# A hybrid attention block on one core: x scaled by ScalarE, its block sums on VectorE, the second burst of each head at job 9, two plain tiles after the last short jobs

## What is computed

```python
h = rmsnorm(x, g_norm)
z = h @ w_in                       # 2048 x 12296: per head q, k, v, gate; 8 forget logits; two merge gates
oa = differential attention of 8 heads (two softmax maps, partial rotary), rmsnorm, * silu(gate)
ob = forgetting attention of 8 heads (cumulative log-forget bias),          * silu(gate)
m = sigmoid(ma) * (oa @ w_proj_a) + sigmoid(mb) * (ob @ w_proj_b)
out = rmsnorm(x + m @ w_out, g_final)
```

## Time and profile before

| | |
|---|---|
| time, median of 3 runs | 762.02 us (760.89 to 762.63) |
| the profiled execution's own time | 762.58 us |
| its span, first to last instruction | 760.6 us |
| TensorE busy | 736.4 us, 97% of the span |
| VectorE, ScalarE, GpSimd busy | 77%, 56%, 14% |
| mean granted clock of TensorE | 0.994 of full speed |

### The profile page before, as it was taken

How to read it: one execution, slowest core, us unless ns; L and a number is a source line. 1 busy time by engine, 2 the same in 40 slices (tenths; PEclk the granted TensorE clock), 3 DMA queues, 4 the chain that set the end, 5 groups by cost and what they waited for, 6 DMA issues and landing times.

```text
span 760.6 us, 9798 instructions
## 1 busy us (share of the span) xinstructions
PE 736.4 (97%) x3536; PEld 611.5 (80%) x3536; DVE 582.7 (77%) x755; ACT 424.2 (56%) x624; POOL 108.4 (14%) x165
## 2 busy tenths in 40 slices
PE   8889999999999999999999999999998899999996
PEld 6678888888888888888887888887777688888886
DVE  6976688789769789778979877988997457665552
ACT  6555665555656565666565565656665343444541
POOL 0660212010000003120303020210020000001110
PEclk9999999999999999999999999999999899999999
DMA  8458646767866676776575767566767455855542
GB/s 321 124 192 280 247 173 218 252 213 265 280 230 222 214 256 230 255 264 221 198 270 193 254 230 285 198 228 204 253 206 246 137 177 198 325 191 190 189 148 111
DMA packets 47374, 168.97 MB, mean 222 GB/s; under 512 B 5400, under 2 KB 5408, under 8 KB 46816
## 3 DMA queue, kind: packets, MB, share of 16 engines
q1 hardware_dynamic: 46064, 164.97, 62.8%
q10 hardware_dynamic: 1008, 1.84, 0.7%
q0 software_dynamic: 256, 1.54, 0.5%
HBM read 166.23 MB, written 2.11 MB: 221 GB/s over the span
## 4 chain that ended last, share of the span: by engine, by line
PE 78%; DVE 11%; issue 3%; ACT 3%; DMA 3%; ACTq 0%; POOL 0%; DVEq 0%; POOLq 0%
PE Z L336 25%; PE Z L338 24%; PE Z L337 24%; DVE w_lo L831 5%; ACT w_hi L606 2%; PE A L438 1%; DMA w_raw<-in_w_main 1%; DMA x_sb<-in_xT 1%; DVE z_sb L884 1%; DVE w_raw L845 1%; DVE x_sb L847 1%; PE A L404 1%; PE B L420 1%; PE Dk L429 1%; PE B L417 1%
## 5 line engine op out<-in xcount | busy, mean ns | idle before, releaser
L831 DVE TENSOR_TENSOR w_lo<-w_raw,w_hi 128x1024 fp32r<-128x1024 f32 (+1 forms) x240 | 293.0, 1226 | 114.6 <-ACT w_hi L606 111.3
L606 ACT ACTIVATE w_hi<-w_raw 128x1024 fp32r<-128x1024 f32 (+1 forms) x235 | 243.7, 1043 | 204.4 <-PE Z L338 156.3
L336 PE MATMUL Z<-w_hi,hT_hi 128*128 128x512 f32 (+2 forms) x720 | 274.9, 382 | 6.5 <-DVE w_lo L831 5.0
L338 PE MATMUL Z<-w_hi,hT_lo 128*128 128x512 f32 (+2 forms) x720 | 272.8, 379 | 0.0
L337 PE MATMUL Z<-w_lo,hT_hi 128*128 128x512 f32 (+2 forms) x720 | 272.8, 379 | 0.0
L336 PEld LDWEIGHTS Z<-w_hi,hT_hi 128*128 128x128 f32 x720 | 135.3, 188 | 34.8 <-issue 6.1
L338 PEld LDWEIGHTS Z<-w_hi,hT_lo 128*128 128x128 f32 x720 | 135.3, 188 | 25.7
L337 PEld LDWEIGHTS Z<-w_lo,hT_hi 128*128 128x128 f32 x720 | 135.4, 188 | 24.4
L336 PE MATMUL Z<-w_hi,sum_hi 128*128 128x512 f32 x256 | 102.9, 402 | 7.0 <-DVE gates L868 5.0
L338 PE MATMUL Z<-w_hi,sum_lo 128*128 128x512 f32 x256 | 100.9, 394 | 0.0
L337 PE MATMUL Z<-w_lo,sum_hi 128*128 128x512 f32 x256 | 100.7, 393 | 0.0
(11 more groups left out here) (184 smaller groups left out, 603.2 us busy)
## 6 DMA issues: line engine op xcount, KB each, us to landing
w_raw<-in_w_main SPq DMA_DIRECT2D x283, 512.0 KB, 4.2
x_sb<-in_w_main SPq DMA_DIRECT2D x16, 512.0 KB, 7.5
w_raw<-in_w_fl SPq DMA_DIRECT2D x8, 264.0 KB, 3.1
o_T<-in_x SPq DMA_DIRECT2D x1, 2048.0 KB, 8.0
x_sb<-in_xT ACTq DMA_DIRECT2D x4, 256.0 KB, 7.9
x_sb<-in_xT SPq DMA_DIRECT2D x4, 256.0 KB, 5.4
gates<-c_rows_dram POOLq DMA_DIRECT2D x1, 1024.0 KB, 6.9
z_sb<-in_g_final SPq DMA_DIRECT2D x1, 1024.0 KB, 10.0
```

The source lines that it names most:

```text
L336: pe.matmul(acc, a_hi, b_hi, start=first, stop=False)
L338: return pe.matmul(acc, a_lo, b_hi, start=False, stop=last)
L606: act.activation(w_hi[:, t % RING, 0:cols_of(t)], weights(t), ACT.Copy).then_inc(hi_ready, 1)
L831: dve.tensor_tensor(w_lo[:, t % RING, 0:n], weights(t), w_hi[:, t % RING, 0:n].bitcast(fp32), ALU.subtract).then_inc(lo_ready, 1)
```

## The change

1. `x` is scaled by g on ScalarE (`x_scale`: 16 operations of 128x256, two after each split of jobs 8 to 15), and the four block sums are made by VectorE (`x_sums`, one after the split of job 18, three between and behind those of jobs 21, 22 and 23). GpSimd's twelve operations are gone.
2. Splitting these sums into `sum_hi`, `sum_lo` (`PARTS_AT`) moves from jobs 21 to 24 to jobs 27, 30, 39 and 46.
3. The burst Y of each head from 3 on moves from step 12 to step 9. What hangs on it moves along.
4. In the last mixed cycle the plain tiles stand at steps 0, 2, 4, 5, 8, 11, 14, 15 (before: 0, 2, 4, 5, 8, 10, 12, 13), the short jobs end at 13 (before: 15).
5. The split of `o_T` moves: part 0 four jobs earlier, parts 2 and 3 to jobs 255 and 256.

```diff
-FOX_STEPS, FOX_SUM_STEPS = (0, 2, 4, 5, 8, 10, 12, 13), (1, 3, 6, 7, 9, 11, 14, 15)
+FOX_STEPS, FOX_SUM_STEPS = (0, 2, 4, 5, 8, 11, 14, 15), (1, 3, 6, 7, 9, 10, 12, 13)
-Y_AT = {25: 0, 33: 1, 43: 2, **{MIXED_JOB + 16 * (b - 2) + 12: b for b in range(3, N_HEADS)}, FOX2_JOB + 5: N_HEADS}
+Y_AT = {25: 0, 33: 1, 43: 2, **{MIXED_JOB + 16 * (b - 2) + 9: b for b in range(3, N_HEADS)}, FOX2_JOB + 5: N_HEADS}
-O_SPLIT_AT = {FOX_JOB - 16: 0, FOX_JOB - 14: 1, FOX_JOB - 6: 2, FOX_JOB + 2: 3}
+PARTS_AT = {PLAIN_JOB + 7: 0, MIXED_JOB + 2: 1, MIXED_JOB + 11: 2, MIXED_JOB + 18: 3}
+O_SPLIT_AT = {FOX_JOB - 20: 0, FOX_JOB - 14: 1, FOX2_JOB + 3: 2, FOX2_JOB + 4: 3}
...
+            def x_scale(j):
+
+                for k in (2 * j, 2 * j + 1):
+                    act.wait_ge(xl_ready, k + 1)
+                    act.activation(xT_sb[:, k, :], xT_sb[:, k, :], ACT.Copy, scale=g_col[:, k:k + 1]).then_inc(h_scaled, 1)
...
                 split(FL_JOB + j)
+                x_scale(j)
...
+            def x_sums(form):
+
+                if form == SUM_1:
+                    dve.wait_ge(h_scaled, KT)
+                    a, b, op = xT_sb[:, near, tok1], xT_sb[:, far, tok1], ALU.add
...
+                dve.tensor_tensor(sums_raw[:, form], a, b, op).then_inc(sums_ready, 1)
...
             split(18)
+            x_sums(SUM_1)
...
             for t in range(PLAIN_JOB, PLAIN_JOB + RING):
                 split(t)
+                if t > PLAIN_JOB:
+                    x_sums((SUM_2, SUM_4, SUM_3)[t - PLAIN_JOB - 1])
...
-            for j in range(TILES):
-                pool.wait_ge(xl_ready, 2 * j + 2)
-                pool.wait_ge(x_squared, j + 1)
-                sl = slice(2 * j, 2 * j + 2)
-                pool.tensor_tensor(xT_sb[:, sl, :], xT_sb[:, sl, :], g_col[:, sl].unsqueeze(2).to_broadcast([P, 2, SEQ]),
-                                   ALU.mult).then_inc(h_scaled, 1)
```

More of the change, by code:

```diff
@@ L754, in _ @@
                 split(job + RING)
-                if PLAIN_JOB + 1 <= job < PLAIN_JOB + 5:
-                    sum_hi_part(job - PLAIN_JOB - 1)
+                if job in PARTS_AT:
+                    sum_hi_part(PARTS_AT[job])
                 attention(job)
@@ L884, in x_sum @@
                 dve.tensor_tensor(x_ssq, before, x_sq[:, 2 * j:2 * j + 2, :], ALU.add).then_inc(x_summed, 1)
+            def x_sums(form):
+                if form == SUM_1:
+                    dve.wait_ge(h_scaled, KT)
+                    a, b, op = xT_sb[:, near, tok1], xT_sb[:, far, tok1], ALU.add
+                elif form == SUM_2:
+                    a, b, op = sums_raw[:, SUM_1], xT_sb[:, near, tok0], ALU.subtract
+                elif form == SUM_4:
+                    a, b, op = xT_sb[:, far, tok0], sums_raw[:, SUM_2], ALU.subtract
+                else:
+                    a, b, op = xT_sb[:, near, tok0], xT_sb[:, near, tok1], ALU.subtract
+                if form in (SUM_2, SUM_4):
+                    dve.wait_ge(sums_ready, form)
+                dve.tensor_tensor(sums_raw[:, form], a, b, op).then_inc(sums_ready, 1)
             dve.memset(warm, 0.0).then_inc(warm_ready, 1)
@@ L1079, in _ @@
                     dve.tensor_scalar(c_neg[:], C[0:HEADS, 0:SEQ], -1.0, None, ALU.mult).then_inc(c_neg_ready, 1)
-                if PLAIN_JOB + 1 <= job < PLAIN_JOB + 5:
-                    sum_lo_part(job - PLAIN_JOB - 1)
+                if job in PARTS_AT:
+                    sum_lo_part(PARTS_AT[job])
                 attention(job)
```

## The result

The changed kernel took 752.69 us (median of 4 runs, 748.14 to 754.77) beside 761.65 us for the kernel before: a ratio of 0.987, 95% interval 0.983 to 0.992. It is faster by 9 us, 1.2%; the forecast was 745.8 us, 741 to 751. The profiled execution took 752.39 us, its span is 750.6 us.

A forecast was written before the change was run, and what follows sets the result against it. TensorE's own rate was taken to bound the steady state. Start 6.1, bursts 2.0 and last mixed cycle 8.1 us sum to 16.2 us off the 762.02 us median: 745.8 us, range 741 to 751 us.

The forecast's parts named there:

- The start: Kernel start, GpSimd's work moved to ScalarE and VectorE: 6.5 us won less a new wait of 0.4 us, 6.1 us.
- first 264-column matmul: Sign at the start: TensorE begins it near 30.3 us instead of 34.01 us, 3.7 us won.
- first 256-column one: Sign at the start: TensorE begins it near 43 us instead of 49.56 us, its wait of 2.81 us gone whole.
- the `c_nat` wait: End of job 21, before the `C` product: VectorE's block sums leave a new wait of 0.4 us.
- The last mixed cycle: Its end: no stop for the fold of P2 before job 252 and no lower clock, 8.1 us won.
- the fold ended 2.2 us ahead of job 252: Last mixed cycle: fold of P2 done 2.2 us before job 252 asks for it, formerly 5.02 us behind.
- The bursts: Burst Y at step 9: 4.5 us of old waits won, 2.5 us of new waits, net 2.0 us.
- The old waits: TensorE's waits at steps 3 and 4 of the next cycle: all go, 3.9 us plus slower first matmuls, 4.5 us.
- The evacuation is late: Next step 0 waits 0.5 us for VectorE's evacuation in cycles 7, 8, 10, 11 and 12: 2.5 us of new waits.
- the one-cycle clock: One differential head's cycle timed from TensorE's end of step 9; put the evacuation 0.3 us late for step 0.
- The slower one: Rival, burst at step 9: every evacuation late in 12 cycles, a loss from 1.6 us each, 767 us at 2 us; 3 in 100.

The follow-up runs named there:

- e4: Kernel before with only x scaled by ScalarE, block sums on VectorE and their later splits: 754.53 us, ratio 0.990.
- e7: Kernel before with only the last mixed cycle's new order of plain tiles and short jobs: 754.11 us, ratio 0.990.
- e1: Changed kernel with burst Y back at step 12, all other edits kept: 745.25 us, ratio 0.977.
- e3: Changed kernel with the differential heads' rotary step cut to one product per head (output lacks the rotation): 743.72 us, ratio 0.975.
- e6: Kernel before with only burst Y moved to step 9: 766.85 us, ratio 1.007.
- e10: Changed kernel with ScalarE evacuating both halves (heads 9 and up) and `combine_maps` four bodies behind Y instead of two: 747.3 us, ratio 0.981.
- e5: Changed kernel with ScalarE evacuating both halves of a differential head's tile (heads 9 and up): 741.71 us, ratio 0.974.
- e8: Changed kernel measured once more, nothing altered: 751.81 us (749.88 to 755.49), ratio 0.987.
- e2: Changed kernel with VectorE's normalizers and `combine_maps` four bodies behind Y instead of two, behind the evacuation: 744.41 us, ratio 0.976.

## Why the prediction was wrong

**The start, 6.1 us forecast: right in mechanism, mis-sized by 1.8 us.** e4 alone gives 7.9 us. `x_sum`, `half_rstd` and the split came back to the lengths that the undisturbed rows gave. TensorE's first 264-column matmul moved by 4.1 us and its first 256-column one by 7.2 us, for 3.7 and 6.5 forecast; 0.46 us of both stood already at 10.7 us, ahead of anything that the change touches. Two terms were mis-sized in the jobs behind: waits of 0.7 us at 56.54 us went too, which I had left out, and the `c_nat` wait, forecast at 0.4 us, measured about 0.1 us. Job 22 starts 7.7 us sooner (61.86 for 69.56). Single traces are good to half a microsecond here: the transposes behind job 21 start at 68.4 to 69.2 us in three kernels with the old start and at 60.7 to 61.9 us in ten with the new one. The extra 1.8 us was luck for the forecast: without it the whole would have been missed by more.

**The last mixed cycle, 8.1 us forecast: right.** e7 gives 7.8 us, and the traces of before and after differ by 7.9 us there. In the changed kernel the fold ended 2.2 us ahead of job 252, as laid out, and the clock held.

**The bursts, 2.0 us forecast: here it failed.** The two terms that stood in the sum were right. The old waits went, 4.9 us by the starts for 4.5 forecast. The evacuation is late in cycles 7, 8, 10, 11 and 12, the five forecast, by 0.46 us four times and 0.66 us once, 2.5 us for 2.5 forecast. (One reading was off without consequence: five of the twelve cycles, not six, have no `combine_maps`.) The step that failed is the one-cycle clock, where "VectorE then does its half" is followed down to the evacuation and no further: TensorE, ScalarE and VectorE were on that clock, and GpSimd was not, although `rope` of the next head waits for that same evacuation and the transposes at step 4 wait for `rope`. Its term was put at nothing without a reason.

What the runs showed in its place: `rope` costs 6.0 us of waits, 6.8 us by the starts of matmuls, and about 1.6 us of lower clock behind one of them. With it the bursts cost some 5.5 us instead of winning 2.0: the lead of the changed kernel's trace is 7.7 us at the transposes at 337.5 us, 2.2 us at those of the last head at 561.0 us, and 10.1 us at the end, behind the fold's 7.9 us; the profiled executions differ by 10.2 us. (The four terms, 4.9 - 2.5 - 6.8 - 1.6, make -6.0 us; the 0.5 us between was not followed.) e1 to e3 show that the missing term is `rope`: each takes the wait away by another road, and each is 7 to 9 us faster than the changed kernel.

The rows needed were in the trace of before: `rope` started right behind the evacuation, at 367.51 us, and ended near 373 us, 8 us ahead of the transposes at 381.0 us. That looks like ample slack. In the changed kernel `rope` starts 1.9 us later against the transposes, and its eight products take 8.1 us more, 11.87 for 3.78: it was mostly their length that used the slack up.

The Trainium skill has the rule for that, in "SBUF — State Buffer", "Who interferes with whom": a VectorE instruction with two inputs in SBUF contends with a GpSimd instruction that reads SBUF, and the pair of ports that the two share is an exclusive lock. The rows agree: a product takes 0.25 us when VectorE pauses or reads PSUM, and 1.18 to 1.23 us in the median beside a row of operations of 1.22 us. They go beyond it in one point: a product can wait past three such operations (3.38 us) or nine (9.59 us in e6). I used this contention for the start, in one direction, where GpSimd slowed VectorE, and did not ask what VectorE's new order does to GpSimd.

Of the rivals none was this one. The slower one named the late evacuation, with 1.6 us per head as the point from which it decides; e6 shows that the burst's move alone is in fact a loss of 4.9 us. The range missed by 1.7 us: it had no room for an engine that was not on the plan.

Open: what decides whether a product of GpSimd gets its turn after one of VectorE's operations or only after three or nine; and why e10 is slower than either of its cures, which only rows of one place suggest.

## What to carry to other kernels

When a burst of work moves, list every engine that waits for any of its results or for what is now queued behind it, the idle engines too: an engine at 14% busy sat on the critical path as soon as its 12 small operations per head ran beside an unbroken row of VectorE's two-input ones. A short wait in such a chain was cured here at its start (e5, 10 us better than the changed kernel in e8) or by putting operations that read PSUM, and a pause, beside the small ones (e2), and the two cures did not add up (e10). The bank last used before a row of long tiles was freed in time by putting other tiles behind its last use (e7), not by an earlier burst (e6).

## What was not expected of the hardware

- A GpSimd product of 128x32 takes 0.25 us when VectorE pauses or reads PSUM (e6: five of them in 1.11 us beside two folds) and 1.2 us beside VectorE's row of operations with both inputs in SBUF. It can wait past more than one of them: 3.38 us in the changed kernel, 9.59 us in e6, and in e3, where one product per head is left, 2.8 us in the median.
- The length of TensorE's stop alone does not tell whether its clock falls. Before the first 256-column matmul it stood 2.81 us in the kernel before and 2.89 us in e6 and kept the full clock, and 3.11 us in e7 and was granted 0.50 from 50 to 53 us. 2.1 us in cycle 11 of the changed kernel were followed by 3.4 us at the lower level. The same stop of 5.02 us for the fold came with 6.8 us of the lower level in the kernel before and 3.4 us in e4.
- The changed kernel, with several stops of 1 to 2 us, varies by 6 us from run to run (748.14 to 754.77, 749.88 to 755.49), the kernel before by 2.4 to 2.7 us in 7 runs, and the kernels without the stops for `rope` by 0.7 to 1.8 us in 4.
